# Gated rows added to their token's row by an accumulating indirect store, with b_down inside the down products

## The reference, cut to what matters

```python
def moe_ffn(h, router_w, router_b, w_gate_up, b_gate_up, w_down, b_down):
    logits = (xt @ router_w + router_b).astype(jnp.float32)
    top_v, top_i = lax.top_k(logits, TOP_K)
    gates = jax.nn.softmax(top_v, axis=-1)
    ...                                # rows sorted by expert, padded to blocks
    def expert_block(args):
        gu = xb @ w_gate_up[e] + b_gate_up[e]
        x_glu = jnp.minimum(gu[:, ::2], SWIGLU_LIMIT)
        x_lin = jnp.clip(gu[:, 1::2], -SWIGLU_LIMIT, SWIGLU_LIMIT)
        act = x_glu * jax.nn.sigmoid(SWIGLU_ALPHA * x_glu) * (x_lin + 1.0)
        return act @ w_down[e] + b_down[e]
    out_buf = out_buf.reshape(P, D) * gate_buf[:, None]
    out = jnp.zeros((T + 1, D), out_buf.dtype).at[tok_buf].add(out_buf)

# the seam, then the second block
x = x + gate2 * rms_norm(y, g_post_ffn[l])      # end of the first block
h = rmsnorm(x, norm_gain[l]); z = h @ w_in[l]   # start of the second
```

## Time and profile before

| | us |
|---|---|
| median of three runs | 1777.77 (1776.94 to 1783.9) |
| the profiled execution | 1778.3 |
| its span | 1776.6 |
| TensorE busy | 1632.0 (92%) |
| DVE busy | 1181.8 (67%) |
| ACT busy | 980.0 (55%) |
| POOL busy | 408.4 (23%) |
| software DMA queue (gathers, stores) | 8256 packets, 18.46 MB, 2.7% of 16 engines' span |
| HBM | 495.2 MB read, 16.8 MB written |

### The profile page before, as it was taken

One profiled execution on the slowest core, in us unless ns is written; L12 is line 12 of the kernel. 1 busy time (PEld: TensorE's weight loads), 2 busy tenths in 40 slices (PEclk: granted clock), 3 DMA queues, 4 the chain that ended last, 5 costly groups with the idle time before them and its releaser, 6 DMA issues. The chain is left out here.

```text
span 1776.6 us, 54864 instructions
## 1 busy us (share of the span) xinstructions
PE 1632.0 (92%) x16793; PEld 852.8 (48%) x16794; DVE 1181.8 (67%) x1932; ACT 980.0 (55%) x1754; POOL 408.4 (23%) x533
## 2 busy tenths in 40 slices
PE   6999889899899999989988899999896889998897
PEld 3888754633334433333432333333331567777853
DVE  5795345667677777767765677777663566955665
ACT  4434533167577777757754677677662453524401
POOL 1000000033234334423431243334231000620000
PEclk9999989899999999999998999999996999999999
DMA  9882224478989999995899999999999922211101
GB/s 340 284 276 79 97 78 197 170 294 366 427 333 388 426 427 426 427 427 211 333 427 427 426 428 417 427 427 404 427 426 427 353 75 72 83 36 51 63 2 48
DMA packets 121954, 508.57 MB, mean 286 GB/s; under 512 B 13635, under 2 KB 42280, under 8 KB 72501
## 3 DMA queue, kind: packets, MB, share of 16 engines
q1 hardware_dynamic: 113332, 488.60, 68.2%
q0 software_dynamic: 8256, 18.46, 2.7%
q10 hardware_dynamic: 290, 0.48, 0.1%
HBM read 495.20 MB, written 16.78 MB: 288 GB/s over the span
## 5 line engine op out<-in xcount | busy, mean ns | idle before, releaser
L2045 DVE COPY ring<-staging 128x1024 f32 (+1 forms) x962 | 653.2, 700 | 285.4 <-SPq L1786 110.8
L1977 ACT ACTIVATE ring<-staging 128x512 f32 (+1 forms) x962 | 592.9, 630 | 330.2 <-SPq L1786 124.1
L1920 PE MATMUL banks<-staging,rowsT 128*32 (+1 forms) x1280 | 600.1, 616 | 61.2 <-DVE ring L2045 59.8
L1920 PE MATMUL banks<-ring,rowsT 128*32 128x512 f32 x3840 | 602.5, 616 | 0.0
L1920 PEld LDWEIGHTS banks<-staging,rowsT 128*32 128x32 f32 x1280 | 127.2, 110 | 452.9 <-issue 443.7
L1943 PE MATMUL banks<-staging,hiddenT 128*32 x1280 | 297.6, 386 | 3.2 <-DVE ring L2045 2.1
L1943 PE MATMUL banks<-ring,hiddenT 128*32 128x256 f32 x3840 | 299.3, 387 | 0.0
L1943 PEld LDWEIGHTS banks<-staging,hiddenT 128*32 128x32 f32 x1280 | 136.8, 112 | 165.0 <-issue 77.1
L1943 PEld LDWEIGHTS banks<-ring,hiddenT 128*32 128x32 f32 x3840 | 152.4, 111 | 0.0
L1920 PEld LDWEIGHTS banks<-ring,rowsT 128*32 128x32 f32 x3840 | 141.2, 110 | 0.0
L2346 PE MATMUL banks<-h3T,w_in_hi 128*128 128x512 f32 (+1 forms) x432 | 131.2, 388 | 0.0
(11 more groups left out here) (434 smaller groups left out, 1947.1 us busy)
## 6 DMA issues: line engine op xcount, KB each, us to landing
staging<-in_w_gate_up SPq DMA_DIRECT2D x256, 1024.0 KB, 12.7
staging<-in_w_down SPq DMA_DIRECT2D x128, 1024.0 KB, 12.5
stage<-in_w_mod SPq DMA_DIRECT2D x22, 1024.0 KB, 5.7
stage<-in_w_in SPq DMA_DIRECT2D x25, 512.0 KB, 3.9
stage<-in_w_in SPq DMA_DIRECT2D x10, 1024.0 KB, 5.6
mixer<-expert_rows SPq DMA_DIRECT2D x6, 1024.0 KB, 10.0
x<-in_x SPq DMA_DIRECT2D x2, 2048.0 KB, 10.4
staging<-in_w_out SPq DMA_DIRECT2D x1, 4096.0 KB, 15.5
```

What stands on the lines that cost most here:

```text
L1920: mm = pe.matmul(k.bank(0)[c * SLOTS:(c + 1) * SLOTS, :], rowsT[:, q % 2, row], w, start=first and q == 0, stop=not first and q == KT - 1, ...
L1977: act.activation(ring[:, pos % RING, BY_ACT], staged(i, e, pos, 3 * PART, PART), ACT.Copy).then_inc(act_filled, 1)
L2045: dve.tensor_copy(ring[:, pos % RING, BY_DVE], staged(i, e, pos, PART, 2 * PART)).then_inc(dve_filled, 1)
```

## The change

- **Gates.** The softmax over the winning logits is worked out at the end of the router stage (ACT `Exp`, DVE sum, reciprocal, product, four copies to `gate4`), and SP writes it to a DRAM table `gate_table` of 2048 x 4. GpSimd fetches 128 gates per unit by an indirect load (`fetch_gate`) and copies them to `gate_now` (`move_gate`), both in `store_rows` behind the store. `read_y` waits for `gate_ready` and scales by `gate_now` as it copies.
- **Sum over choices.** The indirect store goes to `mixed_rows`, one row per token, with `compute_op=ALU.add`. The list that it uses is TOKENS in place of PAIRS. The store before has landed when the next is issued, the last one too (`pool.wait_ge(y_out, 16 * end)` stands ahead of it). The table is zeroed in the attention stage: one DVE memset of 128x1024 and one DMA of 2 MB.
- **b_down.** It is split into three bf16 parts in the router stage (`parts_down`, beside the up bias). Each unit's down products start with four bf16 products 96x256 (`bias_down`), with a tile `pick_below` that DVE makes per unit.
- **Combination.** `gate_e`, the gate split, the diagonal matrices, `weigh`, `add_choices`, and the b_down split go. SP loads one tile of `mixed_rows` (512 KB) and one of x after `last_out` and `over`, four times. DVE multiplies the tile by gate2 (`gate_moe`), ACT squares it, and the rest is as before. `keep_clock` runs 24 products ahead of the wait for `over` and 10, 9, 8 and 4 behind it. Three half projections are done ahead in place of two. Some SBUF buffers (`keep`, `square`, `sa`, `rows_leaving`) have other places.

```diff
             def _(sp):
                 ...
+                sp.wait_ge(zeros_set, 1)
+                sp.dma_start(d["mixed_rows"].rearrange("(t p) n -> p t n", p=P),
+                             zeros.unsqueeze(1).broadcast_to([P, NT, D])).then_inc(zeros_out, 16)
+                sp.wait_ge(zeros_out, 16)
...
                     if n in FORM_AT:
                         if n == 0:
+                            dve.memset(zeros, 0.0).then_inc(zeros_set, 1)
                             dve.wait_ge(gain_in, 16)
...
+                sp.wait_ge(gate_set, 1)
+                for c in range(TOPK):
+                    sp.dma_start(d["gate_table"][c * S:(c + 1) * S].rearrange("(t p) q -> p t q", p=P), k.gate4[:, c]
+                                 ).then_inc(k.gate_out, 16)
...
                 for m in range(PARTS):
                     act.wait_ge(reduced, m)
                     act.activation(parts, raw, ACT.Copy).then_inc(rounded, 1)
+                    act.wait_ge(reduced_down, m)
+                    act.activation(parts_down, raw_down, ACT.Copy).then_inc(rounded_down, 1)
...
+                act.wait_ge(gate_diff, 1)
+                act.activation(k.gates[:], k.gates[:], ACT.Exp).then_inc(gate_exp, 1)
...
+                dve.wait_ge(gate_exp, 1)
+                chain(dve.tensor_reduce(gsum[:], k.gates[:], AX.X, ALU.add))
+                chain(dve.reciprocal(gsum[:], gsum[:]))
+                chain(dve.tensor_tensor(k.gates[:], k.gates[:], gsum[:].unsqueeze(2).broadcast_to([P, NT, TOPK]),
+                                        ALU.mult))
+                for c in range(TOPK):
+                    ins = dve.tensor_copy(k.gate4[:, c], k.gates[:, :, c:c + 1].broadcast_to([P, NT, QUARTERS]))
+                chain(ins)
+                dve.sem_inc(gate_set, 1)
                 dve.wait_ge(slots_ps, NT)
...
-            pool.tensor_copy(k.slot[:, at:at + 1], k.lists[:, PAIRS, slot_list(n)]).then_inc(scatter_ready, 1)
+            pool.tensor_copy(k.slot[:, at:at + 1], k.lists[:, TOKENS, slot_list(n)]).then_inc(scatter_ready, 1)
+
+        def fetch_gate(n):
+
+            pool.tensor_copy(k.slot[:, 5:6], k.lists[:, PAIRS, slot_list(n)]).then_inc(gate_row, 1)
+            pool.wait_ge(gate_row, n + 1)
+            pool.sem_inc(gate_seen, 1)
+            pool.indirect_dma_start(
+                out=gate_land[:, 0:1], out_offset=None, in_=d["gate_table"].rearrange("r (q n) -> (r q) n", q=QUARTERS),
+                in_offset=bass.IndirectOffsetOnAxis(ap=k.slot[:, 5:6], axis=0),
+                bounds_check=NO_ROW - 1, oob_is_err=False).then_inc(gate_in, 16)
+
+        def move_gate(n):
+
+            pool.wait_ge(gate_in, 16 * n + 16)
+            after(pool, y_read, n)
+            pool.sem_inc(gate_free, 1)
+            pool.tensor_copy(gate_now[:, 0:1], gate_land[:, 0:1]).then_inc(gate_ready, 1)
+            pool.wait_ge(gate_ready, n + 1)
+            pool.sem_inc(gate_free, 1)
 
         def scatter_rows(src, at, done):
 
             pool.sem_inc(y_seen, 1)
             pool.indirect_dma_start(
-                out=d["expert_rows"].rearrange("r (c n) -> (r c) n", c=QUARTERS),
+                out=d["mixed_rows"].rearrange("t (c n) -> (t c) n", c=QUARTERS),
                 out_offset=bass.IndirectOffsetOnAxis(ap=k.slot[:, at:at + 1], axis=0), in_=src[:], in_offset=None,
-                bounds_check=NO_ROW - 1, oob_is_err=False).then_inc(done, 16)
+                bounds_check=QUARTERS * S - 1, oob_is_err=False, compute_op=ALU.add).then_inc(done, 16)
...
             scatter_rows(leaving, 3, y_out)
+            move_gate(n + 1)
+            fetch_gate(n + 2)
...
         gather(2, landing, 0, rows_in)
+        pool.wait_ge(k.gate_out, 16 * TOPK)
+        fetch_gate(0)
+        move_gate(0)
+        fetch_gate(1)
         move_rows(2)
...
         pool.wait_ge(scatter_ready, end + 1)
+        pool.wait_ge(y_out, 16 * end)
         pool.wait_ge(y_read, end + 1)
         scatter_rows(y, 4, last_out)
         pool.wait_ge(rows_in, 16 * units + 16)
-        pool.wait_ge(y_out, 16 * end)
+        pool.wait_ge(gate_in, 16 * units + 16)
         pool.sem_inc(k.over, 1)
...
                 if m == 0:
                     pe.wait_ge(hT_ready, n + 1)
                     after(pe, y_read, n)
+                    pe.wait_ge(below_ready, n + 1)
+                    for c in range(QUARTERS):
+                        mm = pe.matmul(k.bank(4)[c * SLOTS:(c + 1) * SLOTS, 0:GLU], pick_below[0:PE_BIAS, :], k.bias_down[0:PE_BIAS, c, :],
+                                       start=True, stop=False)
+                    mm.then_inc(below_used, 1)
...
-            act.activation(y[:], k.bank(4)[:, 0:GLU], ACT.Copy).then_inc(y_read, 1)
+            act.wait_ge(gate_ready, n + 1)
+            act.activation(y[:], k.bank(4)[:, 0:GLU], ACT.Copy, scale=gate_now[:, 0:1]).then_inc(y_read, 1)
...
+        def pick_for_down(n):
+            after(dve, below_used, n)
+            dve.tensor_scalar(pick_below[:], ones[:], k.lane[:, bass.ds(n, 1)], None, ALU.mult
+                              ).then_inc(below_ready, 1)
...
-                load_choices(0)
-                load_choices(1)
-                load_x(k, sp, 2)
-                load_choices(2)
-                load_x(k, sp, 3)
-                load_choices(3)
+                for t in range(NT):
+                    sp.dma_start(moe[t], d["mixed_rows"][t * P:(t + 1) * P, :]).then_inc(moe_in[t], 16)
+                    load_x(k, sp, t)
+                load_slice(k, sp, 2)
...
+                keep_clock(24)
                 pe.wait_ge(k.over, 2)
...
-                weigh(0)
-                weigh(1)
-                weigh(2)
+                pe.wait_ge(moe_in[0], 16)
+                keep_clock(10)
+                pe.wait_ge(x_ready, 1)
+                keep_clock(9)
                 turn_h(0)
-                weigh(3)
+                keep_clock(8)
                 turn_h(1)
+                keep_clock(4)
+                project_ahead(0)
                 turn_h(2)
-                project_ahead(0)
+                project_ahead(1)
                 turn_h(3)
-                project_ahead(1)
+                project_ahead(2)
...
-                def add_choices(t):
-                    ...
+                def gate_moe(t):
+                    dve.wait_ge(moe_in[t], 16)
                     if t == 0:
                         dve.wait_ge(gate2_in, 16)
-                    chain(dve.tensor_tensor(choices[t][:, 2, :], a, k.gate2[:], ALU.mult))
+                    chain(dve.tensor_tensor(gated[t], moe[t], k.gate2[:], ALU.mult))
```

212 lines of the change are left out of this document (66 added, 146 removed).

## The result

The changed kernel takes 1804.8 us in the median of six runs (1802.4 to 1805.5) against 1777.9 for the kernel before (1775.9 to 1783.9): a ratio of 1.0141, 95% interval [1.0125, 1.0157]. It is 27 us slower. The forecast was 1786 with a range of 1767 to 1804, so the direction was right and the size was not: +8 was expected.

The account below looks back on a forecast made before the run. Experts: full DMA engines bound some 60 of 80 units, TensorE paces 19; a serial piece follows. Terms 3.8 + 15.7 + 0 + 2.2 + 0.6 - 14.4 = +7.9 on 1777.8 gave 1786 us, range 1767 to 1804.

Parts of the forecast that it names:

- The accumulating store: Experts' store: adding costs one more DMA pass, 0.27 us a unit; with gate fetch 0.05, 60 units, less slack: 15.7 us.
- the rival of two more passes: Experts' store: the addition costs two more passes, 0.54 us a unit; total +24, 1802 us; chance 0.08.
- The rival of the free addition: Experts' store: the old row is fetched while the next is handled, so no extra time; 1770 us; chance 0.25.
- The slack: Last full-engine experts' stretch: 424 GB/s against 427 leaves 3.5 us that a fuller queue may use at no cost.
- The end of the experts: After the last unit: the last store waits for the one before to land, so SP is released 1.0 us later (0 to 3).
- The combination: After the experts: fewer loads, weighing and sums, and a third half projection (2.6); gain 14.4 us, later SP release included.
- The start: Before the first unit's result: 1.2 us for the gates' softmax, 1.0 for POOL's detour, 0.6 for the attention stage's memset.
- POOL's detour: Start of experts: POOL fetches and copies gate 0 and starts gate 1 before moving unit 2's rows; 1.0 us (0 to 5).
- The bias: Down products: four bias products cost 0.20 us on each of 19 TensorE-paced units, 3.8 us (2 to 7.6).
- GpSimd: Experts: gate work lengthens POOL's round to 11.9 us; 5 us of free lag before TensorE needs the rows covers it; charged 0.
- The rival's last sentence: Rival that GpSimd becomes the pace, 1798 us, chance 0.20: the same if the store takes over 8.5 us to land.
- the 12.6 us round: Experts: POOL's round if new casts and descriptors take long values, 0.9 over the pace; +12, 1798 us; chance 0.20.

Follow-up runs that it names:

- e1: The changed kernel with the plain store, without the addition (the sum over choices left out): ratio 0.9977 to the kernel before.
- e2: The changed kernel without fetching and moving gates on GpSimd and with the read of bank 4 unscaled: ratio 1.0115 to the kernel before.
- f7: The kernel before with the third half projection done ahead and nothing else: ratio 1.0019 to the kernel before.
- e4: The changed kernel without the products with b_down and without DVE's second pick: ratio 1.0155 to the kernel before.
- e5: The changed kernel with only POOL's order at the start altered (unit 2's rows and unit 3's gather before moving gate 0): ratio 1.0121 to the kernel before.
- f6: The changed kernel with the gate multiplied in GpSimd's existing copy, no ACT wait or scale, gate table written behind the border: ratio 1.0188 to the kernel before.
- f1: The kernel before with its store to the table of pairs adding to zeros: ratio 1.0182 to the kernel before.

## Why the prediction was wrong, step by step

The span missed the forecast by 18.4 us (26.3 against 7.9): 11.1 in the middle, 6.1 at the start, 1.2 at the end. In the middle the addition was forecast at 60 x 0.27 - 3.5 = 12.7 us and measured at 28.3, 15.6 too little; bias and gates were forecast at 3.8 and 3.0 and have at most 2.3 together (what e1's middle has over before's), 4.5 too much.

**The accumulating store: the step that failed.** The prediction put the store at 0.27 us a unit and the addition at one more pass, 0.27, "because the old row is as long as the new". The half-width run shows this to be right for the bytes: 0.52 in place of 0.27. What it left out is a part that doesn't go with the bytes, 0.19: an adding packet takes longer whatever its size (27 ns against 10), and the rows no longer travel in packets of four (128 in place of 32 a unit). The addition costs 0.44 us a unit, between the forecast and the rival of two more passes (0.54). This is the term that was mis-sized, and it alone decides the case: with it the change is 1.4% slower, without it 0.2% faster. The rival of the free addition is out.
The Trainium skill ("Collectives: The Full Stack", The bandwidth ceiling: the fold count and why AG ≠ RS ≠ AR) says of a collective's reduce-scatter between cores that its addition needs two source reads, and that it therefore runs at about half the rate of the plain copy. This store is another transfer; its trace agrees for the part that goes with the bytes (0.52 for 0.27), and the 0.19 comes on top.

**The slack: wrong.** The prediction took 3.5 us off because the last stretch ran at 424 GB/s and not 427. The loaded stretch fell by the same share (424 to 411, where 427 fell to 414): there was nothing to use up. So the term is not 60 x 0.32 - 3.5 = 15.7. Removing the addition gave 28.3 us in the middle of the span, 64 units' worth of 0.44, and e2 puts the gate's work at 2. The 60 units were nearly right, and the deduction was not.

**The end of the experts: right in number by luck.** The last store waits for the one before to land, as foreseen. Its descriptors start at 1429.84, 3.9 us after the last read's start where it was 1.3, and SP is released at 1433.65, 7.7 us after that read in place of 7.1 in before and 3.8 in e1:

```profile
1429.84 1.60 POOL L1891 DMA_INDIRECT mixed_rows<-y_rows,eps  x1 [2.29 <-DMA gates<-gate_table,eps]
...
1433.65 0.33 SPq L2300 DMA_DIRECT2D mixer<-mixed_rows  x1
```

The profile puts the wait down to the gate's gather, but the code waits there for the store before and for the read; that store's descriptors started 8.5 us earlier, at 1421.35. The release is 0.7 us later than in before, where 1.0 was forecast. That is the sum of two things: the last store starts 2.7 us later, and SP follows 3.8 us after its start in place of 5.8, which nobody foresaw and no run explains. Against e1 the addition takes some 4 us here too, beside the 28 of the middle.

**The combination: right, with one term too large.** From SP's release to the end it is 1802.9 - 1433.65 = 369.2 us against 1776.6 - 1393.47 = 383.1, 13.9 less, where 15.4 were forecast without the later release. The first multiplication on DVE, the third half projection, DVE's last two pieces of h, and the products behind that half:

```profile
1437.46 1.23 DVE L2560 TENSOR_TENSOR mixer<-mixer,gate_back 128x1024 f32<-128x1024 f32 x1 [4.16 <-DMA mixer<-mixed_rows]
...
1465.27 0.48 PE L2354 MATMUL banks<-h3T,w_in_hi 128*128 128x256 f32 x2
...
1465.74 1.29 DVE L2573 TENSOR_TENSOR h3T<-banks,h3T 128x512 fp32r<-128x512 f32 x2 [1.08 <-ACT h3T L2436]
...
1468.23 0.40 PE L2354 MATMUL banks<-h3T,w_in_hi 128*128 128x256 f32 x2
```

DVE starts 3.8 us behind the release (4 forecast) and is done with its last piece of h at 33.4 (it was 45.9). The products behind the halves start at 34.6 where 34.3 was forecast (47.1 in before; both are still second halves of 256 columns, not yet the full-length ones that the prediction calls them). So 12.6 of the 13.9 us are won ahead of this point and 1.3 behind it, where the third half was to give 2.6. f7 shows no gain from it on the kernel before. In the change it has a place: it runs from 1465.27, and without it TensorE would have waited for h until 1467.03, so it can fill at most 1.8 us. The term was too large, and no run takes the third half out of the change to show what it is worth.

**The start: the term that was missed.** Forecast 1.2 for the softmax, 1.0 for POOL's detour and 0.6 for the memset. The softmax took what was forecast: the lists begin at 344.81 in place of 344.12, and the rows that lead up to it began 0.5 us earlier in this execution, so 1.2. The table's writes, which the text named only as a risk for the range, delay the border by 3.7 us, because the border waits for a gather that queues behind them. POOL's detour was worked out to bring the rows of unit 2 at 367.4 and the softmax's 1.2, so at 368.6. It brought them at 373.2 (372.74 and 0.41); the border, which let go 4.3 us later than in before (354.87 against 350.53, the softmax's part in it), accounts for nearly all of the difference.

**The bias: forecast 3.8, measured none.** The text named the pause in which the products may hide and took the half of a row nevertheless. The TensorE-paced units did get longer, 12.0 us in place of 11.5, near the 11.7 that was named as the sign of the bias; but e4 and e5 show that this is the late read, so the sign would have been met for the wrong reason.

**GpSimd.** The round was forecast at 11.9 us with the lag as cover, and this held: POOL is not the pace in the change (it waits for y in 66 of the units, and e2 gains only 2 us in the middle), and it becomes the pace when about 1 us is added to it behind the store's landing (f6, where the multiplication takes 1.3 us in the median and the copy 0.4). The rival's last sentence, a landing of over 8.5 us, is the form in which it comes.
The Trainium skill ("SBUF — State Buffer", Who interferes with whom) says that GpSimd is blocked for the length of a VectorE copy in a two-port mode that was issued first, and by this the prediction called the 12.6 us round the likely one. The trace of the change shows single operations stretched (the gate's copy takes 1.00 us in the median and 0.18 at its shortest), which would fit, but no run shows that VectorE's copies are the cause, and the round stayed at TensorE's pace.

## What to carry to other kernels

Where the DMA engines are full, an addition in a store is not free: count the bytes twice, and add a fixed time for each packet, since small rows that travelled in fours go singly (here 0.52 and 0.19 us a unit in place of 0.27). What it saves (here an end that is 13 us shorter, and 18 in e1) is won once, and what it costs is paid with every unit that DMA time bounds. Tiny writes ahead of a border that waits for a transfer delay that border (here by 3.7 to 4.7 us); moving them behind it gave back 0.7 us of this, because the next gather then waited for them.

## What the runs showed of the hardware

An indirect store of a unit's rows (128 places of 1 KB, 102 of them filled in the mean) kept the 16 DMA engines for 0.27 us, the same store with an addition for 0.71, and one of half the width with the addition for 0.45. In packets: 159 ns for a plain one of 4 KB, 101 for an adding one of 1 KB, 64 for an adding one of 512 bytes. POOL's descriptors for it took 1.77 us in the median (1.75 in f1) in place of 1.07, and in f6 the cast that waits for its landing began 9.2 to 10.9 us after the descriptors' start. The bytes that the page counts for it are the same with and without the addition, so only the packets and the queue's share show it. Four bf16 products of 96x256 between two groups of f32 products took no time of their own: 0.55 us from the last group to the next with them and 0.56 without.
